# Key and query turns of the latent mixer dealt out over the memory value projection, and the rope queries' squares set behind the first key copies

## The reference, cut to what matters

```python
c_q, c_kv, k_r, q_mem = jnp.split(h @ mla_w_in[j], MLA_SPLITS, axis=-1)
q = (rmsnorm(c_q, q_norm) @ w_uq).reshape(B, S, MLA_HEADS, MLA_NOPE + MLA_ROPE)
kv = (rmsnorm(c_kv, kv_norm) @ w_ukv).reshape(B, S, MLA_HEADS, MLA_NOPE + MLA_DV)
q_nope = rmsnorm(q[..., :MLA_NOPE], qn_norm)
q_rope = apply_rope(rmsnorm(q[..., MLA_NOPE:], qr_norm), cos, sin)
k_nope = rmsnorm(kv[..., :MLA_NOPE], kn_norm)
k_rope = apply_rope(rmsnorm(k_r, kr_norm)[:, :, None, :], cos, sin)
o = causal_block_attention(concat(q_nope, q_rope), concat(k_nope, k_rope), v, scale)
# beside it, over the memory:
k, v = jnp.split(mem_h @ w_kv, 2, axis=-1)
o_mem = softmax(rmsnorm(q_mem) @ rmsnorm(k).T * scale) @ v
x = x + jnp.concatenate([o, o_mem], axis=-1) @ w_out[i]
```

## Time and profile before

| | |
|---|---|
| median of 3 runs | 1651.74 us (1651.64 to 1653.42) |
| profiled execution: span | 1651.0 us |
| TensorE (PE) busy | 1626.6 us, 99% |
| VectorE (DVE) busy | 1204.9 us, 73% |
| ScalarE (ACT) busy | 957.9 us, 58% |
| GpSimd (POOL) busy | 96.4 us, 6% |
| stretch of the memory value projection | 805.21 to 826.77 us |
| granted TensorE clock, 800 to 850 us | 1.00 |

### The profile page before, as it was taken

How to read it: one execution, slowest core, us unless ns; L and a number is a source line. 1 busy time by engine, 2 the same in 40 slices (tenths; PEclk the granted TensorE clock), 3 DMA queues, 4 the chain that set the end, 5 groups by cost and what they waited for, 6 DMA issues and landing times.

```text
span 1651.0 us, 25472 instructions
## 1 busy us (share of the span) xinstructions
PE 1626.6 (99%) x9240; PEld 1409.9 (85%) x9240; DVE 1204.9 (73%) x1729; ACT 957.9 (58%) x1539; POOL 96.4 (6%) x113
## 2 busy tenths in 40 slices
PE   9999999999999999999999999999999999999998
PEld 8888897788888888888788888896888878688886
DVE  6897687578776688765877887657787649768763
ACT  5665454555654466545865665457665546856652
POOL 0000012000000010002500100000000001000000
PEclk9999999999999999999999999999999999999999
DMA  7656545345656556644425556551466654236661
GB/s 274 218 186 218 171 163 170 115 153 167 194 187 216 172 190 199 217 166 159 161 97 172 186 196 217 178 179 64 154 192 190 215 179 153 86 119 204 191 217 63
DMA packets 79208, 286.77 MB, mean 174 GB/s; under 512 B 8833, under 2 KB 9217, under 8 KB 78865
## 3 DMA queue, kind: packets, MB, share of 16 engines
q1 hardware_dynamic: 77904, 281.12, 52.1%
q0 software_dynamic: 752, 3.67, 0.6%
q10 hardware_dynamic: 464, 0.82, 0.2%
HBM read 284.53 MB, written 1.05 MB: 173 GB/s over the span
## 4 chain that ended last, share of the span: by engine, by line
PE 94%; ACT 2%; DVE 2%; issue 1%; DMA 0%; POOL 0%; SPq 0%; DVEq 0%; ACTq 0%; POOLq 0%
PE ps L2352 28%; PE ps L2358 14%; PE ps L2234 13%; PE ps L2295 13%; PE ps L2299 6%; PE ps L2331 3%; PE ps L2332 3%; PE ps L2333 3%; PE ps L2166 1%; PE ps L2870 1%; PE ps L2843 1%; ACT prob L1336 1%; PE ps L2824 1%; PE ps L2394 1%; PE ps L2397 1%
## 5 line engine op out<-in xcount | busy, mean ns | idle before, releaser
L1430 DVE TENSOR_TENSOR wlo<-raw,whi 128x1024 fp32r<-128x1024 f32 x532 | 646.5, 1224 | 177.2 <-ACT whi L899 175.9
L899 ACT ACTIVATE whi<-raw 128x1024 fp32r<-128x1024 f32 x532 | 553.9, 1053 | 243.5 <-PE ps L2299 125.1
L2352 PE MATMUL ps<-acts,whi 128*128 128x512 f32 x2016 | 483.2, 391 | 0.3 <-DVE prob L1596 0.3
L2352 PEld LDWEIGHTS ps<-acts,whi 128*128 128x128 f32 x2016 | 370.4, 188 | 72.4 <-DVE prob L1596 0.5
L2358 PEld LDWEIGHTS ps<-acts,wlo 128*128 128x128 f32 x2016 | 258.3, 191 | 9.7
L2358 PE MATMUL ps<-acts,wlo 128*128 128x256 f32 x2016 | 262.1, 283 | 0.0
L2234 PE MATMUL ps<-whi,acts 128*128 128x512 f32 (+3 forms) x772 | 220.4, 369 | 3.0 <-ACT arena L993 2.5
L2295 PE MATMUL ps<-hids,whi 128*128 128x512 f32 x704 | 176.3, 392 | 0.0
L1596 DVE TENSOR_TENSOR prob<-ps,prob 128x512 f32<-128x512 f32 x132 | 91.0, 690 | 99.8 <-ACT prob L1040 99.6
L2234 PEld LDWEIGHTS ps<-whi,acts 128*128 128x128 f32 x772 | 140.5, 188 | 26.7 <-issue 6.2
L2295 PEld LDWEIGHTS ps<-hids,whi 128*128 128x128 f32 x704 | 126.7, 189 | 22.6
(11 more groups left out here) (272 smaller groups left out, 1698.7 us busy)
## 6 DMA issues: line engine op xcount, KB each, us to landing
raw<-units SPq DMA_DIRECT2D x532, 512.0 KB, 4.2
arena<-mem_in POOLq DMA_DIRECT2D x2, 1024.0 KB, 7.4
x<-x_in SPq DMA_DIRECT2D x4, 256.0 KB, 5.3
arena<-mem_in POOLq DMA_DIRECT2D x4, 256.0 KB, 5.2
out<-x SPq DMA_DIRECT2D x4, 256.0 KB, 2.1
const<-const_in ACTq DMA_DIRECT2D x1, 560.0 KB, 3.3
row<-row_in POOLq DMA_DIRECT2D x1, 512.0 KB, 7.5
row<-row_in ACTq DMA_DIRECT2D x1, 134.0 KB, 3.5
```

The lines of the kernel that those rows point to most:

```text
L899: nc.scalar.activation(whi[:, u % RING, :], raw[:, u % RAW, :], ACT.Copy).then_inc(hi_ready, 1)
L1430: V.tensor_tensor(wlo[:, u % RING, :], raw[:, u % RAW, :], whi[:, u % RING, :].bitcast(F32), ALU.subtract).then_inc(lo_ready, 1)
L2352: T.matmul(ps[:, bank, :], whi[:, slot, w], acts[:, k].rearrange("p e s -> p (e s)"), start=k == 0, stop=False)
```

## The change

On TensorE the turns of keys and position-free queries are no longer made in two blocks ahead of tiles 1 and 4, but two heads at a time: the rotary key and keys 0 and 1 ahead of tile 0, keys 2 and 3, 4 and 5, 6 and 7 ahead of tiles 1, 2 and 3, queries 0 to 3 ahead of tile 4, queries 4 and 5 ahead of tile 6, queries 6 and 7 ahead of tile 7, in front of the rotated queries. The memory scores stay ahead of tile 5. The waits for all turns taken (`all_taken`) in front of keys and rotated queries are gone; those of `turn` itself stay. On ScalarE the copies follow the new order, the squares of the rope queries (`squares_of(square_q, m_qr, ...)`, L1002) go behind the copies of keys 0 and 1, and the four weight splits stand one at a time between the copies. The last split stays behind the last copy. VectorE's, POOL's and SP's code is not touched.

```diff
--- before.py
+++ after.py
@@ -1268,14 +1268,20 @@
                     self.split(2)
                     after_queries = self.ea
                     self.evacuate(2, m_v, CROSSED, "ckv")
+                    self.take_key_halves()
+                    keys = [(by_tile(m_kT[:, h, :]), GAIN_AT["mla_kn_norm"]) for h in range(MH)]
+                    at = GAIN_AT["mla_qn_norm"]
+                    queries = [(m_k[:, :, h * P:(h + 1) * P], at) for h in range(MH)]
+                    self.take(keys[0:2])
                     act.wait_ge(ss_dve, STAT["memk1"][1])
                     self.squares_of(square_q, m_qr, after_queries)
-                    self.split(1)
-                    self.take_key_halves()
-                    self.take([(by_tile(m_kT[:, h, :]), GAIN_AT["mla_kn_norm"]) for h in range(MH)])
-                    self.split(2)
-                    at = GAIN_AT["mla_qn_norm"]
-                    self.take([(m_k[:, :, h * P:(h + 1) * P], at) for h in range(MH)])
+                    self.take(keys[2:4])
+                    self.split(1)
+                    self.take(keys[4:6])
+                    self.split(1)
+                    self.take(keys[6:8] + queries[0:4])
+                    self.split(1)
+                    self.take(queries[4:8])
                     self.split(1)
                     self.g += 2
 
@@ -2695,18 +2701,17 @@
                     self.project([0, 1, 2], 512, MIDDLE, 2, between={1: lambda: self.memory_keys(1)}, taken=False)
                     self.project([3, 4], 1024, CROSSED, taken=False)
 
-                    def keys():
-                        self.ready_rows(2)
-                        self.all_taken()
-                        self.turn([[m_kr2[:, t, :] for t in range(TT)]])
-                        self.turn(turn_tiles(m_k, MH))
-
-                    def position_free_queries():
-                        self.turn(turn_tiles(m_qn, MH))
+                    def keys(first, last):
+                        if first == 0:
+                            self.ready_rows(2)
+                            self.turn([[m_kr2[:, t, :] for t in range(TT)]])
+                        self.turn(turn_tiles(m_k, MH)[first:last])
+
+                    def position_free_queries(first, last):
+                        self.turn(turn_tiles(m_qn, MH)[first:last])
 
                     def rotated_queries():
                         self.ready_rows(1)
-                        self.all_taken()
                         self.turn(turn_tiles(m_qr, MH // 2))
 
                     def first_scores():
@@ -2714,8 +2719,14 @@
                             self.bank_free(b)
                         self.scores_of_jobs(memory_jobs(1), range(XH))
 
+                    def last_turns():
+                        position_free_queries(6, 8)
+                        rotated_queries()
+
                     self.project(MEMORY, 512, NARROW, 2, taken=False,
-                                 between={1: keys, 4: position_free_queries, 5: first_scores, 7: rotated_queries})
+                                 between={0: lambda: keys(0, 2), 1: lambda: keys(2, 4), 2: lambda: keys(4, 6),
+                                          3: lambda: keys(6, 8), 4: lambda: position_free_queries(0, 4), 5: first_scores,
+                                          6: lambda: position_free_queries(4, 6), 7: last_turns})
                     self.order = ORDER_MLA
                     self.attention(memory_jobs(1) + mla_jobs(), XH)
 
```

## The result

The changed kernel takes 1657.61 us on the median of six runs (1656.07 to 1659.20), the one before, run beside it, 1652.68 (six runs, three of them those of the 1651.74 ahead of the prediction): +4.9 us, ratio 1.003 (95% interval 1.002 to 1.004). The forecast was +4.3, and 1656.0 us as a time.

What follows compares the result with a forecast made beforehand. TensorE, busy 99% of the span, was taken as the bound. Late ScalarE copies +3.2, attention's end -0.3 and slow clock +1.4 gave +4.3 us on the median 1651.74: 1656.0 us, range 1652.6 to 1658.0 (forecast's own 1654.8 to 1657.2).

Steps and rivals of the forecast that it cites:

- ScalarE's last copies: Last split, table load and exponentials queue behind the copy of queries 6 and 7; TensorE resumes at 829.93, +3.2 us.
- The table load's drain: Extra 1.38 us per ScalarE table switch by the skill, left out of the forecast; 1% for the drain alone.
- The clock: After 5.5 us idle, TensorE falls to 1.2 GHz 4.8 us after its last matmul, for 3.4 us: 1.4 us lost.
- rival 4: Clock low for two stretches, or table load costs its drain too: +2.9 + 3.1, 1657.7 us; 4%, 1% for drain alone.
- The 0.3 us given back at the attention's end: VectorE is delayed 0.3 less than TensorE, so up to 0.3 of TensorE's 0.36 us wait for ScalarE at 847.94 goes.
- POOL's release of VectorE at 819.12: VectorE waits for POOL until 819.12, then is busy without a gap until its last rope query copy ends at 826.58.
- Rival 3: ScalarE is not late; VectorE's chain remains and TensorE gains at most 0.2 us, 1651.5 us; 15%.
- The rival that the saving passes through: TensorE finishes the projection 3 us earlier and goes on to head 0's scores, 1648.7 us; 5%.

Runs made afterwards that it cites:

- Experiment 1: Changed kernel with queries 4 to 7 turned ahead of the memory scores instead of ahead of tiles 6 and 7; 1651.12 us, 1652.43 before the change.
- 2: Changed kernel with a one-column exponential ahead of the copies of queries 4 to 7, loading ScalarE's table early; 1655.78 us, 1652.43 before the change.
- 3: Changed kernel with the last pair of rope query turns made eight times, filling TensorE's idle time; 1655.57 us, 1652.43 before the change.
- 4: Changed kernel with rope query squares and one weight split back in front of the rotary key's copies on ScalarE; 1659.98 us, 1652.43 before the change.
- 5: Experiment 1's kernel with VectorE's copies of the turned rope queries one step earlier; 1650.48 us, 1652.08 before the change.
- 6: Kernel of 5 with VectorE's two weight splits moved from before head 0's maximum to the attention's end; 1651.10 us, 1652.08 before the change.
- 9: Kernel of 6 with the memory values evacuated from PSUM earlier on ScalarE and VectorE; 1650.41 us, 1652.57 before the change.
- 10: Kernel of 5 with the memory values evacuated earlier, VectorE's two splits kept before head 0's maximum; 1651.34 us, 1652.57 before the change.
- experiment 7: Kernel before with only ScalarE's part: rope query squares behind copies of keys 0 and 1, following split behind all key copies; 1654.32 us against 1652.08.
- 8: Experiment 1's kernel with the squares and one split back in their old place on ScalarE; 1651.46 us, 1652.08 before the change.

## Why the prediction was right

- **ScalarE's last copies** (+3.2 forecast, +3.01 in the trace). The chain came as worked out: queries 6 and 7 turned 16.3 us into the stretch (forecast 16.4), from there to the table load 2.1 us, then exponentials, `scaled(0)`, a maximum, `scaled(1)`, copies, and TensorE 0.06 us behind their end. Experiment 1 removes it by one move and 2 shortens it by the load's 1.28 us and a little more: shown, not only argued.
- **The table load's drain**, which the Trainium skill, ScalarE: Activation LUTs, What ACT_TABLE_LOAD costs, puts at some 1.38 us more, does not show: the load begins 0.02 us after the split before it, and the first exponential 0.01 us after its end (822.17 + 1.28, then 823.46).
- **The clock** (1.4 forecast, 1.5 measured by 3). That the clock falls behind the idle time was right, and it fell when forecast, 4.8 us after TensorE's last matmul (823.30, then 828.1). That it was one stretch of 3.4 us was luck in part: in 4 the clock fell 3.7 us after the last matmul, was low for 6.8, and the same idle time cost 2.7. The condition that the idle time has to be longer than those 4.8 us was wrong: in 2 it was 3.7, and the cost was 1.7.
- **The time itself.** The median of 1657.61 lies above the forecast's own range (1654.8 to 1657.2) and next to rival 4's 1657.7, two slow stretches. The profiled execution has one. 0.9 of the 1.6 us by which it misses 1656.0 is the kernel before, whose median rose from 1651.74 to 1652.68 with three more runs; against the kernel beside it the forecast of +4.3 is 0.6 short.
- **The 0.3 us given back at the attention's end** was wrong. The wait for ScalarE there is still 0.36 us, in all twelve traces, and begins each time right behind TensorE's own turns of that job's probabilities: ScalarE copies those, so it does not hang on how far VectorE is.
- **POOL's release of VectorE at 819.12, taken as unchanged,** was wrong by 1.2 us (12.72 us into the stretch for 13.91). In the changed kernel that is hidden behind the 4.45 us wait for exponentials; in 1 it is most of the gain. Rival 3, which gave TensorE at most 0.2 us if ScalarE was not late, is built on that release: 1 meets its condition and gained 1.5.
- **The rival that the saving passes through** failed as said: the stalls in the projection did go (tile 0 to tile 7 without a wait over 0.5 us, the projection done 19.45 us into the stretch for 21.72), and came back as 5.12 us at the next place.

## What to carry to other kernels

When work is dealt out over a longer stretch, look at what its last piece releases: here the last four copies stood in front of a split, a table load and all exponentials, and 2.3 us saved in the projection became a 5 us stall. Deal out from the front and leave the last piece where it was. A long idle time on TensorE is to be charged with the half clock behind it (1.5 to 2.7 us for 3.7 to 5.1 us here), and work that changes nothing can be cheaper than idleness, as in 3. The next wait in line should be read from a trace each time. In experiments 5, 6, 9 and 10 each wait removed was followed by another one, and though TensorE begins head 0's scores 1.5 us earlier in 9 than in 1 (18.54 us into the stretch for 20.03), it ends only 0.5 earlier.

## What the runs showed of the hardware

- The clock fell to 1.2 GHz behind idle times of 3.7 (experiment 2) and 5.1 us (the changed kernel and 4), and also in experiment 7 in the last of four idle pieces of 1.3, 0.5, 0.2 and 1.1 us that lie within 7 us; it stayed at 1.00 behind 2.05 (3) and 1.33 us (1). It was low for 3.4 us, or in 4 for 6.8. With 3.7 us of idle time it fell only after work had begun again.
- Some of POOL's short operations took longer beside VectorE's. The 128x16 product at L730 took 1.00 us in the kernel before and 0.73 in 1, where VectorE was splitting, and 0.22 in 8, where VectorE was idle. The first operation of the statistics shows it on both engines, here before (first pair of rows) and changed (second pair):

```profile
808.54 1.07 POOL L721 TENSOR_SCALAR means<-sums 128x16 f32<-128x16 f32 x1
807.27 3.40 DVE L1430 TENSOR_TENSOR wlo<-raw,whi 128x1024 fp32r<-128x1024 f32 x2
...
807.23 0.21 POOL L721 TENSOR_SCALAR means<-sums 128x16 f32<-128x16 f32 x1
807.43 2.38 DVE L1436 TENSOR_TENSOR wlo<-raw,whi 128x1024 fp32r<-128x1024 f32 x2
```

Where POOL's operation falls into VectorE's two splits, it is 0.86 us longer and the splits 1.02. From the start of this operation to the end of the last one (L738) POOL takes 10.49 us before and 9.25 in the changed kernel; in 8, where the first is again 1.07 and the short ones behind it are short, 9.24. So the 1.2 us are spread over several operations and depend on what VectorE does beside them. What makes them slow was not isolated.
